# Chunk loop of a gated delta rule: inverse in quarter products, value pages summed by TensorE, key-query products moved

## The reference, cut to what matters

```
L     = strictly lower part of (k_beta k^T * decay)
t_inv = inverse of (I + L)                # triangular, 128 x 128 for each head
v_new = t_inv (v_beta - (k_beta exp(g)) S)
o     = q_dec S + (q k^T * decay) v_new
S     = S exp(g_last) + k_dec^T v_new
```

## Time and profile before

| what | value |
|---|---|
| median of 3 runs | 2699.7 us (2698.36 to 2700.04) |
| profiled execution | 2699.58 us |
| its span, first to last instruction | 2697.7 us |
| mean granted TensorE clock | 0.996 |
| TensorE busy, whole span | 2643.7 us (98%) |
| VectorE busy, whole span | 1613.4 us (60%) |
| ScalarE busy | 1142.9 us (42%) |
| GpSimd busy | 1346.6 us (50%) |
| the chunk loop's steps | from about 572 us to 761 us of the span |

### The profile page before, as it was taken

One profiled execution on the slowest core, in us unless ns is written; L12 is line 12 of the kernel. 1 busy time (PEld: TensorE's weight loads), 2 busy tenths in 40 slices (PEclk: granted clock), 3 DMA queues, 4 the chain that ended last, 5 costly groups with the idle time before them and its releaser, 6 DMA issues.

```text
span 2697.7 us, 44937 instructions
## 1 busy us (share of the span) xinstructions
PE 2643.7 (98%) x16109; PEld 2443.7 (91%) x16109; DVE 1613.4 (60%) x3290; ACT 1142.9 (42%) x1771; POOL 1346.6 (50%) x613
## 2 busy tenths in 40 slices
PE   8989999989999999999999999999999999999998
PEld 5986666689966899999999999999999999999998
DVE  5227768889977342333337885378863788634323
ACT  2227739844424343334333434343343433444433
POOL 0200025610000666667666676676766767666663
PEclk9999999999999999999999999999999999999999
DMA  5220067634584444444444444444445444444553
GB/s 182 75 87 9 17 177 227 189 98 138 158 260 143 132 142 140 141 141 139 138 138 140 138 138 130 140 143 136 139 132 145 130 141 140 135 132 141 149 156 95
DMA packets 457186, 368.87 MB, mean 137 GB/s; under 512 B 15501, under 2 KB 400114, under 8 KB 456732
## 3 DMA queue, kind: packets, MB, share of 16 engines
q1 hardware_dynamic: 444846, 347.05, 43.5%
q0 software_dynamic: 2992, 12.26, 1.5%
q10 hardware_dynamic: 9174, 7.22, 0.9%
HBM read 351.17 MB, written 17.14 MB: 137 GB/s over the span
## 4 chain that ended last, share of the span: by engine, by line
PE 67%; DVE 3%; ACT 1%; issue 1%; DMA 0%; SPq 0%; POOL 0%; DVEq 0%; ACTq 0%
PE bank L2874 21%; PE bank L2876 21%; PE bank L2875 21%; PE bank L2366 4%; DVE bank L3455 1%; DVE tmp L2742 1%; ACT tmp L2734 1%; DMA big<-in_cache_attn_v 0%; PE bank L2750 0%; PE bank L3658 0%; PE bank L2386 0%; DVE hh L3412 0%; DVE hl L3413 0%; DVE bank L3411 0%; PE bank L1772 0%
## 5 line engine op out<-in xcount | busy, mean ns | idle before, releaser
L3333 POOL TENSOR_TENSOR wl<-wring,wh 128x1024 fp32r<-128x1024 f32 x466 | 1137.4, 2456 | 589.5 <-ACT wh L3090 589.3
L2874 PE MATMUL bank<-xh,wh 128*128 128x344 f32 x2688 | 862.9, 321 | 0.3 <-POOL wl L3333 0.3
L2876 PE MATMUL bank<-xh,wl 128*128 128x344 f32 x2688 | 859.1, 320 | 0.0
L2875 PE MATMUL bank<-xl,wh 128*128 128x344 f32 x2688 | 857.5, 319 | 0.0
L3090 ACT ACTIVATE wh<-wring 128x1024 fp32r<-128x1024 f32 x466 | 484.2, 1055 | 765.5 <-PE bank L2876 657.4
L2874 PEld LDWEIGHTS bank<-xh,wh 128*128 128x128 f32 x2688 | 505.8, 188 | 1.8 <-POOL wl L3333 0.6
L2876 PEld LDWEIGHTS bank<-xh,wl 128*128 128x128 f32 x2688 | 505.3, 188 | 0.0
L2875 PEld LDWEIGHTS bank<-xl,wh 128*128 128x128 f32 x2688 | 504.2, 188 | 1.2
L3411 DVE TENSOR_TENSOR bank<-bank,gates_tmp 128x344 f32<-128x344 f32 x132 | 69.2, 524 | 510.8 <-PE bank L2876 423.6
L3455 DVE SCALAR_TENSOR_TENSOR bank<-big,vec,bank 128x344 f32<-128x344 f32 (+1 forms) x696 | 355.3, 575 | 0.5
L2874 PE MATMUL bank<-hh,wh 128*128 128x344 f32 x1040 | 334.5, 322 | 3.5 <-DVE hl L3413 3.5
(11 more groups left out here) (439 smaller groups left out, 3263.5 us busy)
## 6 DMA issues: line engine op xcount, KB each, us to landing
wring<-in_ffn_w_down SPq DMA_DIRECT2D x132, 512.0 KB, 3.5
wring<-in_ffn_w_gate SPq DMA_DIRECT2D x131, 512.0 KB, 3.9
wring<-in_ffn_w_up SPq DMA_DIRECT2D x131, 512.0 KB, 3.9
wring<-in_conv_w_pw SPq DMA_DIRECT2D x72, 512.0 KB, 3.9
big<-in_cache_attn_k SPq DMA_DIRECT2D x128, 256.0 KB, 3.0
big<-in_cache_attn_v SPq DMA_DIRECT2D x128, 256.0 KB, 2.9
wring<-in_w_in SPq DMA_DIRECT2D x20, 512.0 KB, 4.1
park<-res_a SPq DMA_DIRECT2D x1, 4128.0 KB, 12.7
```

Of the source, the lines that this page charges most:

```text
L2874: pe.matmul(bank_out, h, mh, start=(n == 0), stop=False)
L2875: pe.matmul(bank_out, h, ml, start=False, stop=False)
L2876: mm = pe.matmul(bank_out, l, mh, start=False, stop=(n == len(terms) - 1))
L3333: pool.tensor_tensor(wl[s % 6][:, :], raw_w[s % WQ] if raw is None else raw, wh[s % 6][:, :].bitcast(F32), ALU.subtract).then_inc(w_cut, 1)
```

## The change

1. **Inverse in quarters.** `left`, `right` and `right_turned` call a new helper `blocks`. Below the last level it issues, for each head, two products of 64 x 64 x 64, on the quarters (0, 0) and (64, 64) of the 128 x 128 matrices. At the last level it issues one 64 x 64 x 64 product for each head, on the corner that is used. The results go to the same PSUM banks as before.
2. **Pages on TensorE.** Samples 0 to 5 are summed in 24 groups of four pages, three groups a step. `page_group` multiplies for each page q of a group a weight block of 32 columns (of which 4 are the page's) by the page's 512 columns, into partitions 32q to 32q + 31 of one bank. It runs after the key transposes (bank 5), after `left(k, 1)` (bank 6) and after `left(k, 2)` (a bank of chunk k - 1). `group_copy` on VectorE copies or adds the bank into one of two buffers, `strip_sum`. `page_column` then multiplies these by a column of `fold`, which picks the head's row out of each strip. TensorE waits for pages (`page_in`) where VectorE did before. The 32 late pages stay on VectorE.
3. **Key-query products moved.** `keys_queries(k)` stands before `turn_values(k)` in a step, not behind it.
4. New waits: TensorE waits in `page_group` for the bank's last reader and in `first`, `values_new` and `outputs` for `group_in`; VectorE waits for `LN + 1` on `l2_inv` in step 8.

```diff
@@ class gdn_in, page_sum
-            if g % PG == 0 and 2 <= b < 6:
-                dve.wait_ge(samp_full, b - 1)
-            if g:
-                dve.wait_ge(vpage_used, 8 + g)
+            dve.wait_ge(vpage_used, 8 + g)
-                w, d = aw_flat[:, at:at + 1], pacc[b][:, h, :]
+                w, d = aw_flat[:, at:at + 1], pacc[b - LATE // PG][:, h, :]
...
-        pacc = 3 * [over(tmp_flat, 0), over(tmp_flat, 1)] + [over(k_last, 0), over(k_last, 1)]
+        pacc = [over(k_last, 0), over(k_last, 1)]
+        HALF = P // 2
-        PAGES = (0,) + 8 * (12,)
-        LATE = sum(PAGES)
+        STRIPS = 4
+        GROUPS = 3 * NB
+        LATE = STRIPS * GROUPS
-        KK, VT, QK, KT = 1, 2, 3, 4
+        strip_sum = [flat(16 * TT, H, P), flat(16 * TT + 512, H, P)]
+        KK, QK, VT, KT = 1, 2, 3, 4
...
         def page_column(pe, b, n):
-            pe.wait_ge(vpage_used, 8 + PG * (b + 1))
+            strips = b < LATE // PG
+            if strips:
+                pe.wait_ge(group_in, PG // STRIPS * (b + 1))
+            else:
+                pe.wait_ge(vpage_used, 8 + PG * (b + 1))
+            part = strip_sum[b % 2] if strips else pacc[b - LATE // PG]
             for h in range(H):
-                mm = pe.matmul(bank[:, n, h:h + 1], pacc[b][:, h, :], ones[:, 0:1], start=True, stop=True)
+                mm = pe.matmul(bank[:, n, h:h + 1], part[:, h, :], fold[:, h:h + 1] if strips else ones[:, 0:1], start=True, stop=True)
             mm.then_inc(samp_full, 1)
+        def page_group(pe, g, n):
+            b, at = g * STRIPS // PG, g * STRIPS
+            for q in range(STRIPS):
+                pp, u = (at + q) % PG // 2, q % 2
+                if u == 0:
+                    pe.wait_ge(page_in[pp % 4], b * 64 + 512 + 32 * (pp // 4 + 1))
+            for q in range(STRIPS):
+                pp, u = (at + q) % PG // 2, q % 2
+                w = aw_flat[:, (at + q) * H:(at + q) * H + 32]
+                mm = pe.matmul(bank[32 * q:32 * (q + 1), n, :], w, ring[:, pp % 4, u, :], start=True, stop=True)
+            mm.then_inc(vpage_used, STRIPS)
+        def group_copy(dve, g, n):
+            b = g * STRIPS // PG
+            dve.wait_ge(vpage_used, 8 + STRIPS * (g + 1))
+            d, src = strip_sum[b % 2].rearrange("p h e -> p (h e)"), bank[:, n, :]
+            if g % (PG // STRIPS) == 0:
+                if b >= 2:
+                    dve.wait_ge(samp_full, b - 1)
+                else:
+                    dve.wait_ge(bias_io, 64)
+                dve.tensor_copy(d, src).then_inc(group_in, 1)
+            else:
+                dve.wait_ge(group_in, g)
+                dve.tensor_tensor(d, d, src, ALU.add).then_inc(group_in, 1)
...
+            def blocks(out, lhsT, rhs, lv, corner):
+                for h in range(H):
+                    if lv < NL - 1:
+                        for r in (0, HALF):
+                            t = slice(r, r + HALF)
+                            mm = pe.matmul(out[t, h, t], lhsT[t, h, t], rhs[t, h, t], start=True, stop=True)
+                    else:
+                        k, m = (slice(r, r + HALF) for r in corner)
+                        mm = pe.matmul(out[m, h, k], lhsT[k, h, m], rhs[k, h, k], start=True, stop=True)
+                return mm
@@ left, right, right_turned (each its four-head loop of full products)
+                blocks(own(c, 0), lnT[c % 2], inv[c % 2], lv, (0, HALF)).then_inc(x_full[c % 2], 1)
+                blocks(own(c, 0), inv_t[c % 2], xm[c % 2], lv, None).then_inc(p_full[c % 2], 1)
+                blocks(own(c, 1), xm[c % 2], inv_t[c % 2], lv, (HALF, 0)).then_inc(p_full[c % 2], 1)
@@ chunk_pe, a step
                 left(k - 1, 3)
+                keys_queries(k)
                 turn_values(k)
-                keys_queries(k)
...
                 turn_keys(k)
+                if k < NB:
+                    pe.wait_ge(attn_done, k + 1)
+                else:
+                    pe.wait_ge(vn_copied, k - 1)
+                page_group(pe, 3 * (k - 1), 5)
...
                 left(k, 1)
                 if k == NB:
                     on_sum(pe, 2, ON_BANK[2])
+                    pe.wait_ge(oc_copied, k - 1)
+                else:
+                    pe.wait_ge(k_scaled, k + 1)
+                page_group(pe, 3 * (k - 1) + 1, 6)
...
+                pe.wait_ge(group_in, 3 * k - 2)
                 values_new(k - 1)
                 left(k, 2)
+                page_group(pe, 3 * (k - 1) + 2, 2 * ((k - 1) % 2) + 1)
+                pe.wait_ge(group_in, 3 * k - 1)
                 outputs(k - 1)
@@ chunk_dve, a step: the calls page(k, 0) to page(k, 12) go
                 corrected(k - 1)
-                page(k, 3)
+                group_copy(dve, 3 * (k - 1), 5)
...
                 decays(k + 1)
+                group_copy(dve, 3 * (k - 1) + 1, 6)
                 join(k, 1)
...
                 lower(k + 1)
-                page(k, 12)
+                group_copy(dve, 3 * (k - 1) + 2, 2 * ((k - 1) % 2) + 1)
```

More of the change, by code:

```diff
@@ L1623, in build @@
         samp_full, sacc_done = sem("samp_full"), sem("sacc_done")
-        PAGES = (0,) + 8 * (12,)
-        LATE = sum(PAGES)
+        STRIPS = 4
+        GROUPS = 3 * NB
+        LATE = STRIPS * GROUPS
         SAMPLE_AT = {2: 0, 4: 1, 5: 2, 6: 3, 8: 4}
-        KK, VT, QK, KT = 1, 2, 3, 4
+        group_in = sem("group_in")
+        strip_sum = [flat(16 * TT, H, P), flat(16 * TT + 512, H, P)]
+        KK, QK, VT, KT = 1, 2, 3, 4
         def set_at(c, what):
@@ L1910, in first @@
                     pe.wait_ge(inv_up[c % 2], ps(c - 2, NL - 1, True))
+                    pe.wait_ge(group_in, 3 * (c - 1))
                 for h in range(H):
@@ L1926, in left @@
                     pe.wait_ge(inv_up[c % 2], ps(c, lv - 1, False))
-                for h in range(H):
-                    mm = pe.matmul(own(c, 0)[:, h, :], lnT[c % 2][:, h, :], inv[c % 2][:, h, :], start=True, stop=True)
-                mm.then_inc(x_full[c % 2], 1)
+                blocks(own(c, 0), lnT[c % 2], inv[c % 2], lv, (0, HALF)).then_inc(x_full[c % 2], 1)
             def right_ready(c, lv):
@@ L1941, in right @@
                 right_ready(c, lv)
-                for h in range(H):
-                    mm = pe.matmul(own(c, 0)[:, h, :], inv_t[c % 2][:, h, :], xm[c % 2][:, h, :], start=True, stop=True)
-                mm.then_inc(p_full[c % 2], 1)
+                blocks(own(c, 0), inv_t[c % 2], xm[c % 2], lv, None).then_inc(p_full[c % 2], 1)
             def right_turned(c, lv):
@@ L1949, in right_turned @@
                 right_ready(c, lv)
-                for h in range(H):
-                    mm = pe.matmul(own(c, 1)[:, h, :], xm[c % 2][:, h, :], inv_t[c % 2][:, h, :], start=True, stop=True)
-                mm.then_inc(p_full[c % 2], 1)
+                blocks(own(c, 1), xm[c % 2], inv_t[c % 2], lv, (HALF, 0)).then_inc(p_full[c % 2], 1)
             def keys_state(c):
@@ L2181, in chunk_dve @@
         def chunk_dve(dve, step):
-            def page(k, n):
-                if n < PAGES[k]:
-                    page_sum(dve, sum(PAGES[:k]) + n)
             def decays(c):
@@ L2304, in chunk_dve @@
             for k in range(1, NB + 1):
-                page(k, 0)
                 pairs(k)
                 join(k - 1, 3)
-                page(k, 1)
                 weights(k)
                 join_turned(k - 1, 3)
-                page(k, 2)
                 corrected(k - 1)
-                page(k, 3)
+                group_copy(dve, 3 * (k - 1), 5)
                 join(k - 1, 4)
                 join(k, 0)
-                page(k, 4)
                 join_turned(k - 1, 4)
                 join_turned(k, 0)
-                page(k, 5)
-                page(k, 6)
                 join_turned(k - 1, 5)
                 if k == NB:
-                    dve.wait_ge(l2_inv, LN)
+                    dve.wait_ge(l2_inv, LN + 1)
                     dve.tensor_tensor(e_qk, e_qk, l2_few.rearrange("p (k b) -> p k b", k=2 * H), ALU.mult).then_inc(l2_out, 1)
@@ L2329, in chunk_dve @@
                 decays(k + 1)
+                group_copy(dve, 3 * (k - 1) + 1, 6)
                 join(k, 1)
-                page(k, 7)
-                page(k, 8)
                 join_turned(k, 1)
-                page(k, 9)
-                page(k, 10)
                 join(k, 2)
@@ L2338, in chunk_dve @@
                 join_turned(k, 2)
-                page(k, 11)
                 lower(k + 1)
-                page(k, 12)
+                group_copy(dve, 3 * (k - 1) + 2, 2 * ((k - 1) % 2) + 1)
                 if k in SAMPLE_AT:
```

## The result

The changed kernel takes 2680.5 us (median; 2677.1 to 2680.6) against 2699.6 for the kernel before on the same chip, ratio 0.9926 (95% interval 0.9906 to 0.9945). A fourth execution took 2917.6 us at a granted clock of 0.845 (0.995 and 0.996 in the others) and is left out of the range and the ratio. Run again later (e9), the same kernel took 2677.3 us (2676.7 to 2679.2) against 2699.3, ratio 0.9917 (0.9903 to 0.9930). It is faster by 19 to 22 us; the forecast was 2683.8, 15.8 us faster than its base.

The account below looks back on a forecast made before the run. TensorE's back-to-back queue was taken to bound the chunk loop. From 2699.6 us, 13.8 for the loop and 2.0 behind it were subtracted, with 0 ahead of it, giving 2683.8 us; range 2676 to 2708.

Parts of the forecast that it names:

- What bounds the kernel: Chunk loop: TensorE's back-to-back queue sets the step, with a little waiting for joins behind VectorE's page sums.
- Quarter products: Inverse in the loop: quarters run in pairs, 0.48 us a group against 0.895, taking 7.1 us a step off TensorE.
- Rival B: Inverse: a product's two quarters do not run together, 0.96 us a group, about 2733 us; chance 0.15.
- Form changes: TensorE in the loop: each change of tile form loses 0.12 to 0.20 us, 2.9 us a step, page column 0.35 more.
- Page groups and VectorE: Loop: three groups of 0.86 us add 2.6 us a step to TensorE; VectorE falls from 22.7 to some 11.5.
- Key-query products: Loop: standing before the value transposes, they hide 0.5 us of the transposes' wait for the state.
- The sum: Loop steps of 22.0 us, 22.75 with a page column, against 24.0 and 24.9; 13.8 us gained.
- the schedule of after: Loop queues followed in the changed order: 173.9 us from first mark to loop's end, against 187.7 before.
- Behind the loop: After the loop: page loads and sums come 2 to 4 us earlier; 2.0 us gain taken, 2.9 at most.
- Ahead of it: Stage before the loop: quarters gain at most 3.7 us, less some 1.3 for form changes and clock lapses; 0 taken.
- C: Loop: short gaps and half-filled quarters make TensorE's clock lapse; ten lapses give about 2700 us; chance 0.12.
- D: Loop: dearer form changes or more waiting than scheduled; 1.5 times the loss gives 2695 us; chance 0.08.

Follow-up runs that it names:

- e9: The changed kernel itself, unchanged, run again later: 2677.3 us, ratio 0.9917 to the kernel before.
- e2: The changed kernel with full 128x128x128 products in the inverse, page strips and moved key-query products kept: 2712.3 us, ratio 1.0042 to the kernel before.
- e1: The kernel before with the quarter products alone, pages on VectorE and key-query products in their old place: 2701.7 us, ratio 1.0002 to the kernel before.
- e3: The changed kernel with each quarter group issuing four products on one tile, then four on the other: 2702.0 us, ratio 1.0006 to the kernel before.
- e11: The changed kernel with the left products of levels 3 and 4 in full products again: 2681.7 us, ratio 0.9941 to the kernel before.
- e7: The changed kernel with the page column alone moved behind `right_turned(k, 1)`, right ahead of `values_new`: 2677.3 us, ratio 0.9914 to the kernel before.
- e12: The changed kernel with the second page group of every step cut to 32 of 512 columns: 2683.7 us, ratio 0.9938 to the kernel before.
- e8: The changed kernel with `keys_queries(k)` put back behind `turn_values(k)`: 2682.3 us, ratio 0.9934 to the kernel before.
- e5: The changed kernel with chunk 0's levels 0 to 2, ahead of the loop, in full products: 2676.6 us, ratio 0.9912 to the kernel before.
- e10: The changed kernel with chunk 0's levels 0 to 2 in full products and the page column right ahead of `values_new`: 2675.5 us, ratio 0.9907 to the kernel before.
- e4: The changed kernel with the page column right ahead of `values_new` and the second page group behind `keys_keys`: 2687.4 us, ratio 0.9953 to the kernel before.
- e6: e1 plus three groups a step of useless strip products on TensorE, results unread: 2697.0 us, ratio 0.9991 to the kernel before.

## Why the prediction was right, point by point

**What bounds the kernel.** Right. Before, TensorE's queue sets the step with VectorE close behind. Taking the page sums off VectorE and putting them on TensorE costs 12 us (e2), with steps of 26.5 and 27.2 us as TensorE's sum has them. Relieving TensorE alone gains nothing (e1): it then waits for VectorE, and the clock falls. Of the kernels run, only those with both parts are clearly faster.

**Quarter products.** 0.060 us a record was taken, 0.0583 measured; 0.48 a group, 0.467 measured. Rival B is excluded: the two quarters write one bank and run together, against the rule of the Trainium skill that the prediction named (TensorEngine Tiling (Array Packing), Gotcha 1). Here the measurement decides. e3 shows that it takes the alternating order. What each quarter saves is seen from e2 to the changed kernel: 4.8 us a step with all form changes paid (26.5 and 27.2 against 21.7 and 22.4).

**Form changes.** 0.145, 0.20, 0.15 and 0.12 were taken; 0.144, 0.20, 0.152 and 0.12 measured between ends. (For strips gives 0.14; the lower 0.12 was taken and came.) That they are paid in time and not hidden is shown by e11 (0.32 to 0.35 us a step, where hidden changes would leave 0.86) and, for 0.25 of 0.345 us, by e7.

**Page groups and VectorE.** 0.86 us a group was taken, 0.88 measured; VectorE 11.5 us a step, 11.9 measured. That no pass is late was wrong once: `outputs` in step 8 waits 1.3 us. What the prediction did not see is that the groups cost less than their length. The second one stands in a gap that ScalarE's copies leave; cut to nearly nothing it gives back 0.20 us, and a wait of 0.53 stands in its place (e12).

**Key-query products.** 0.5 us a step was taken for the hidden wait; undoing it costs 0.64 (e8).

**The sum.** Steps of 22.0 and 22.75 were forecast, 21.7 and 22.4 came. For the loop 13.8 us were forecast and 15.45 came. From the first mark to the end of the loop's last product, as the prediction counts it, the schedule of after has 173.9 us and the trace 173.6; for the kernel before it has 187.7 and the trace 189.1. So the term mis-sized is the base: a difference of two schedules left out 1.4 us of the kernel before, and the schedule of after should have been set against the measured loop. That 173.9 fits so well is in part luck. No term has the 3.2 us of lower clock at the loop's start; the first step took 23.05 us where e5 and e10, whose clock is up by then, took 21.6. The other steps were up to 0.4 us shorter than forecast, which hid it. Behind the loop 2.0 was taken, 2.3 measured. Ahead of it I took 0; 2.1 came, less 0.8 in the stages before. This last I can't attribute: the stretch has 22.2 to 26.0 us in the runs, with lapses of the clock at different places, and the start of it moves between 545.0 and 554.9 us in kernels whose code up to there is the same. Its size is within what the starts and lapses vary by there.

**The rivals.** C did not happen to the changed kernel: behind the first 3.2 us the clock is 1.00 through the loop, as forecast. But its chance of 0.12 rested on too narrow an idea of it. I thought of thinner work (85% streaming in place of 95%) as the danger, and in the changed kernel the thinner work alone did no harm. The kernel stands close to an edge all the same: e4, with the same products in another order and a wait of 0.72 us in seven steps, has lapses in two steps, and e12, with thinner work and waits of 0.53, in four. In e1, where nothing fills the waits for VectorE, the lapses take the whole gain of the quarters. That more work in TensorE's queue can keep the clock up and less can bring it down is shown by e6 and e12; by which property of the queue is not. D did not happen.

**Open.** Which quantity decides whether the clock falls. The busy column doesn't rank the kernels: over 595 to 720 us the filled one (e6) has TensorE busy for 113 of 125 us and keeps its clock, the short-group one (e12), whose slow records count long, for 120 and loses it. The waits don't rank them either. From 595 to 740 us e8 has 5.7 us of them, five of 0.8, and no lapse; e6 has waits up to 1.2 us and no lapse; e12 has 4.7 us, five of 0.5, and four lapses. The windows of e8 and of e12:

```profile
595.00:720.00 125.00, 119.81 (x1966) 95.94 (x1964) 66.81 (x176) 62.38 (x231) 13.10 (x15) 1.00 0.55 157
...
595.00:720.00 125.00, 120.14 (x1875) 99.43 (x1875) 63.18 (x167) 58.72 (x216) 11.79 (x14) 0.93 0.52 146
```

Open too is why the changed kernel has the fall at 769 us and e7 not: their waits there (0.8 and 0.3 us in its two profiles, 0.4 in e7's) are alike.

## What to carry to other kernels

When two engines are both nearly full, cost the parts of a change alone and together: here they are worth +1 and +12 us alone and some -20 together. Before work is taken off TensorE, look for what will stand in the gap: a wait may take its place, and if the clock comes down with it, that costs more than the work did (e12), and a busy column won't show it. Count form changes as instructions of 0.12 to 0.20 us each: a small tile that stands alone between full products saved 0.16 of the 0.43 us of its records.

## What the runs showed of the hardware that was not expected

- Two 64x64 tiles on the diagonal, writing different rows and columns of one PSUM bank, run in pairs: 7 ns between the two, 58 ns from pair to pair.
- In the order of four and four, the second tile starts only with the fifth record of the first, 0.28 us late.
- Products on different tiles can start out of the queue's order: in the changed kernel a corner product starts at 648.32 us and a product of the group ahead of it in the queue at 648.36.
- Adding 24 us of useless products to TensorE's queue made the loop 11.8 us shorter (e6), and cutting one page group a step to a sixteenth of its columns made it 6.3 us longer (e12 against e9); the granted clock over 595 to 720 us went from 0.89 to 1.00 in the one and from 1.00 to 0.93 in the other.
